# The rotary embedding's row exchange in a hybrid decoder layer: by small SBUF transfers instead of a product on TensorE

## The chip, the cores and the metric

The kernel runs on one core of one Trainium2 chip. The metric is the device time in microseconds (us) of one execution; the time shown for a kernel is the median of several executions.

## The reference

One decoder layer on a sequence of 512 tokens with 1024 features, all in float32: a SwiGLU half step, a mixer, a second SwiGLU half step, a final RMSNorm. The mixer projects the normalised input once, runs a gated delta rule (GDN, 4 heads of 128) beside a sparse attention (8 query heads in 2 key groups, head size 64), and joins them in an output projection. Queries and the keys of two of the three attention branches get a partial rotary embedding on their first 16 features:

```python
def partial_rope(x, pos):
    half = ROPE_DIM // 2          # 8
    ...
    x1, x2 = xr[..., :half], xr[..., half:]
    rot = jnp.concatenate([x1 * cos - x2 * sin, x2 * cos + x1 * sin], axis=-1).astype(x.dtype)
    return jnp.concatenate([rot, x[..., ROPE_DIM:]], axis=-1)
```

## The kernel before

Features lie on the 128 partitions and tokens on the free axis. Five engine programs (TensorE as PE, VectorE as DVE, ScalarE as ACT, GpSimd as POOL, SyncE as SP for the loads) run side by side and meet at semaphores. Each engine executes its own list strictly in order. Large products are made of three TensorE passes on split operands (`three_pass`, L592 to L594).

The mixer has three parts. First come seven full projection steps (`pe_projection`). Then comes a mixed stretch whose order is written out in `SCHEDULE`: 14 half projection tiles (`pe_half(n, g)`, each cut into three groups g) alternate with the rounds of the GDN's chunk algorithm (`pe_gdn`, jobs with names such as `g_arg`, `rb`, `kk`, `c1`, `y1`, `t1`, `u1`, `k_tok`, `v_tok`, `vn0`, `s0`, `o`). The third part is the attention. In the mixed stretch the half tiles are there so that TensorE has work while another engine brings the result of a GDN job out of PSUM for the next one.

GDN jobs write to three PSUM banks in turn. A job waits until the job three before it has been evacuated (`gdn_bank_free`). So `v_tok` of the fourth token tile waits for the evacuation of `t4` (DVE, L2250), since the jobs in between are `u4` and `v_tok` of the third tile.

Six tiles are rotated: r = 0, 1 are the two keys (`z[:, 0]`, `z[:, 1]`), r = 2 to 5 the four query tiles (`nq`). A rotated tile holds two groups of 64 features, of which the first 16 are rotated. The source tile r is written by DVE at the end of half tile r + 4 (`dve_half_end`, L1505 or L1507, which signals `proj_evac`). The rotation stands in the schedule behind group 1 of half tile r + 5:

- TensorE multiplies the source with a constant 128 x 128 permutation `rope_swap` (`pe_rope`, L1520). It exchanges rows 0 to 7 with rows 8 to 15 of each group, with a minus sign on one of the two, and gives zero in all other rows. The result lies in bank r % 2.
- DVE makes source x cos (`dve_rope`, L1526), then bank x sin into `z[:, 2 + r % 2]` (L1530), then the sum of both (L1533).
- Half tiles 6 to 11 on TensorE wait (`rope_b`) until L1530 has read that bank.

The constant cos is 1 and sin is 0 outside of the rotated rows. The step on SP that matters here is `sp_mixer`: loads of weight tiles, of eight pieces of the compression weights (L1323), and of the output weights (L1356, L1360). ACT rounds a half tile's weights in `act_half_split` (L1388), and DVE makes the rest in `dve_half_split` (L1394). In front of `SCHEDULE`, ACT copies three constants to bfloat16 (L2428 to L2430).

Of the kernel before, what the change touches and what calls it, by code (L numbers as in the profile page):

```python
# [270 lines left out]
def build(nc, dram, out):  # L271
    with ExitStack() as ctx:
# [4 lines left out]
        def sem(name):  # L277
            return ctx.enter_context(nc.semaphore(name))
# [228 lines left out]
        kqv_ready = sem("kqv_ready")  # L507
        kqv_sq = sem("kqv_sq")
        l2_done = sem("l2_done")
        rope_mm = sem("rope_mm")  # L510
        rope_a = sem("rope_a")
        rope_b = sem("rope_b")
        rope_ready = sem("rope_ready")
# [811 lines left out]
        def sp_mixer(sp):  # L1325
            for m in range(FULL_STEPS):
                step = MIX0 + m
                sp.wait_ge(lo_ready, step - 1)
                if FULL_KIND[m] == "small":
                    sp.dma_start(raw[:, m % 2, 0:KT * P], dram["w_small"]).then_inc(raw_landed[m % 2], 16)  # L1330
                else:
                    sp.dma_start(raw[:, m % 2, :], dram["w_in"][FULL_TILE[m], :, :])\
                      .then_inc(raw_landed[m % 2], 16)
            for s in range(HALF_STEPS):
                par = HALF_LOAD[s][0]
                if s < 2:
                    sp.wait_ge(lo_ready, HALF0 + s - 1)
                elif s == 2:
                    sp.wait_ge(half_lo, 2)
                else:  # L1340
                    sp.wait_ge(half_lo, 2 * s)
                sp.dma_start(raw[:, par, :], dram["w_in"][HALF_TILE[s], :, :]).then_inc(raw_landed[par], 16)
                for piece in {2: (0, 1), 3: (2, 3, 4), 4: (5, 6, 7)}.get(s, ()):
                    if piece == 0:
                        sp.wait_ge(half_lo, 4)
                    elif piece >= 2:
                        sp.wait_ge(cmp_done, piece - 1)
                    sp_cmp(sp, piece)
            for o in range(OUT_STEPS):
                if o < RING:  # L1350
                    sp.wait_ge(cmp_done, 2 * CMP_STEPS) if o == 0 else sp.wait_ge(half_lo, HALVES_N)
                else:
                    sp.wait_ge(lo_ready, splits(OUT0 + o) - 1)
                here = raw[:, o % 2, :].rearrange("p (b k n) -> p b k n", b=2, k=KT)
                rows = dram["w_out"][o, :, :].rearrange("p (b k n) -> p b k n", b=2, k=KT)
                sp.dma_start(here[:, :, 0:4, :], rows[:, :, 0:4, :]).then_inc(raw_landed[o % 2], 16)  # L1356
                for g in range(2):
                    for r in range(2):
                        for b in range(2):
                            sp.dma_start(half_of(here, g)[:, b, 4 + r:8:2, :],  # L1360
                                         rows[r * NSA_DH:(r + 1) * NSA_DH, b, 4 + 2 * g:6 + 2 * g, :])\
                              .then_inc(wout_landed[o % 2], 16)
# [79 lines left out]
        def pe_half(pe, n, g):  # L1442

            if g == 0:
                pe.wait_ge(half_lo, n + 1)
                if n == 0:
                    pe.wait_ge(proj_evac, CONV_EVACS - 2)
                if n in (2, 3):
                    pe.wait_ge(v_evac, n - 1)
                elif n in (4, 5):  # L1450
                    pe.wait_ge(cmp_in_ready, 2 * (n - 3))
                elif n >= 6:
                    pe.wait_ge(proj_evac, CONV_EVACS + n - 5)
                if 6 <= n <= 11:
                    pe.wait_ge(rope_b, n - 5)
            a, b = KGROUPS[g]
            if n < 2:
                for t, k in V_ORDER[2 * a:2 * b]:
                    if n == 0 and (t, k) == (0, 0):
                        pe.wait_ge(proj_evac, CONV_EVACS)  # L1460
                    tok, w = slice(t * P, (t + 1) * P), slice((4 * n + k) * 2 * P, (4 * n + k + 1) * 2 * P)
                    mm = three_pass(pe, banks[t][:, 0:2 * P], h_hi[:, 4 * n + k, tok], h_lo[:, 4 * n + k, tok],
                                    w_hi[:, 1, w], w_lo[:, 1, w], n == 0 and k == 0, n == 1 and k == 3)
                if b == KT:
                    mm.then_inc(half_done, 1)
                return
            for k in range(a, b):
                mm = three_pass(pe, banks[n % 2][:, :], *slot_w(1, (n % 2) * KT + k), h_hi[:, k, :], h_lo[:, k, :],
                                k == 0, k == KT - 1)
            if b == KT:  # L1470
                mm.then_inc(half_done, 1)
# [40 lines left out]
            if n + 2 < HALVES_N:  # L1512
                dve_half_split(dve, n + 2)

        def rope_bank(r):
            return banks[r % 2]

        def pe_rope(pe, r):
            pe.wait_ge(proj_evac, CONV_EVACS + r + 1)
            pe.matmul(rope_bank(r)[:, :], const("rope_swap"), rope_source(r)[0],  # L1520
                      start=True, stop=True).then_inc(rope_mm, 1)

        def dve_rope(dve, r):
            src, dst = rope_source(r)
            dve.wait_ge(proj_evac, CONV_EVACS + r + 1)
            dve.tensor_tensor(dst, src, const("cos"), ALU.mult).then_inc(rope_a, 1)  # L1526
            dve.wait_ge(rope_mm, r + 1)
            if r >= 2:
                dve.wait_ge(rope_ready, r - 1)
            dve.tensor_tensor(z[:, 2 + r % 2, :], rope_bank(r)[:, :], const("sin"), ALU.mult).then_inc(rope_b, 1)  # L1530
            dve.wait_ge(rope_a, r + 1)
            dve.wait_ge(rope_b, r + 1)
            dve.tensor_tensor(dst, dst, z[:, 2 + r % 2, :], ALU.add).then_inc(rope_ready, 1)  # L1533

        def act_projection(act):
            for m in range(FULL_STEPS):
# [857 lines left out]
        def pe_mixer(pe):  # L2394
            pe_projection(pe)
            for what, *n in SCHEDULE:
                if what == "half":
                    pe_half(pe, *n)
                elif what == "scalars":
                    pe_scalars(pe)  # L2400
                elif what == "rope":
                    pe_rope(pe, *n)
                elif what == "cmp":
                    pe_cmp(pe, *n)
                elif what == "hid_sum":
                    pe_hid(pe)
                elif what == "kcvc":
                    pe_kcvc(pe)
                elif what == "scores":
                    pe_scores(pe, *n)  # L2410
                elif what == "cmp_pt":
                    pe_cmp_pt(pe, *n)
                elif what == "att":
                    pe_attention(pe, *n)
                elif what == "gdn":
                    for tt, name in ROUNDS[n[0]]:
                        pe_gdn(pe, tt, name)
            pe_out(pe)

        def act_mixer(act):  # L2420
            act_split(act, MIX0 + 1)
            act.wait_ge(rest_landed, 48)
            act_rms(act, 1)
            act_r(act, 1)
            act_projection(act)
            act_scalars_end(act)
            act_gdn(act, 0, "g_arg")
            act.activation(ident_bf[:, :], ident, ACT.Copy).then_inc(consts_bf, 1)  # L2428
            act.activation(neg_causal_bf[:, :], const("neg_causal"), ACT.Copy).then_inc(consts_bf, 1)
            act.activation(zero_bf[:, :], ident, ACT.Copy, scale=0.0).then_inc(consts_bf, 1)  # L2430
            for what, *n in SCHEDULE:
                if what == "half_end":
                    act_half_end(act, *n)
                elif what == "hid_sum":
                    act_hid_parts(act)
                    act_hid(act)
                elif what == "softmax" and n[0] == 2:
                    act_cmp_exp(act)
                elif what == "cmp_pt":
                    act_cmp_pt(act, *n)  # L2440
                elif what == "gdn_rms":
                    act_gdn_rms(act)
                elif what == "att":
                    act_attention(act, *n)
                elif what == "gdn":
                    for tt, name in ROUNDS[n[0]]:
                        if (tt, name) != (0, "g_arg"):
                            act_gdn(act, tt, name)
            act_out(act)
            act_ffn_start(act, 1)  # L2450
# [30 lines left out]
        def pool_mixer(pool):  # L2481
# [3 lines left out]
            pool.memset(hid_v, 0.0).then_inc(pads_set, 1)  # L2485
            pool.memset(bdv, 0.0).then_inc(pads_set, 1)
            pool.memset(state, 0.0).then_inc(state_ready, 1)
            for what, *n in SCHEDULE:
                if what == "att":
                    pool_scale(pool, *n)  # L2490
# [199 lines left out]
```

## Time and profile before

| | |
|---|---|
| median of 3 executions | 1116.54 us (1116.14 to 1116.83) |
| the profiled execution's own time | 1116.19 us |
| its span in the trace | 1114.4 us |
| PE busy | 1082.6 us, 97% |
| DVE, ACT, POOL busy | 778.0, 446.5, 443.5 us |
| mean granted TensorE clock | 0.989 |

The span is what the profiler records between the first and the last instruction; 1.8 us of the execution's time lie around it. All positions below are us from the start of the span. Busy shares are averages over stages with different limits. A wait is put down to the engine whose signal came last.

### The profile page before, as it was taken

What the parts mean: (1) busy time and instruction counts of PE and PEld (TensorE: products, weight loads), DVE (VectorE), ACT (ScalarE), POOL (GpSimd) and SP (SyncE); (2) the same over time, 40 slices, a digit from 0 to 9 for tenths busy, and PEclk for the clock granted to TensorE, in tenths of its full rate; (3) what the DMA queues carried; (4) which work ended last, traced back from release to release, by engine and by line L of the source; (5) the groups of instructions that cost most, each with busy time, mean ns of one, the idle gap of its engine ahead of it and who ended that gap; (6) DMA issues with size and microseconds to landing.
All of it is one profiled execution on the core that took longest, in us unless ns stands there. A gap on an engine that the chain in (4) does not pass through costs nothing.

```text
span 1114.4 us, 20141 instructions
## 1 busy us (share of the span) xinstructions
PE 1082.6 (97%) x8484; PEld 938.2 (84%) x8484; DVE 778.0 (70%) x941; ACT 446.5 (40%) x639; POOL 443.5 (40%) x281
## 2 busy tenths in 40 slices
PE   6899999999999999999999999999999999999996
PEld 5799899988998888887787667888898899989986
DVE  5998379946987566653566487566997389837964
ACT  6534244423435334311214566343453145413432
POOL 0663169505833000312300389433480279306912
PEclk9999999999999999999999899999999999999999
DMA  6244233333232222113103001123133323422222
GB/s 228 77 124 151 76 94 99 116 108 103 89 112 95 87 103 76 40 58 134 39 28 86 4 1 39 36 79 103 59 104 115 111 77 114 135 92 80 101 85 76
DMA packets 34590, 98.45 MB, mean 88 GB/s; under 512 B 3664, under 2 KB 10320, under 8 KB 32848
## 3 DMA queue, kind: packets, MB, share of 16 engines
q1 hardware_dynamic: 34224, 97.26, 26.7%
q8 instruction: 57, 0.93, 0.3%
q14 instruction: 21, 0.17, 0.0%
q10 hardware_dynamic: 288, 0.08, 0.0%
HBM read 95.24 MB, written 2.10 MB: 87 GB/s over the span
## 4 chain that ended last, share of the span: by engine, by line
PE 87%; DVE 8%; ACT 3%; issue 2%; DMA 0%; POOL 0%; DVEq 0%; ACTq 0%
PE bank L592 25%; PE bank L594 24%; PE bank L593 24%; PE bank L2131 3%; PE bank L1917 1%; PE bank L1884 1%; PE bank L1905 1%; DVE hb_lo L716 1%; DVE w_lo L1020 1%; PE bank L2183 1%; DVE cv L1611 1%; DVE w_lo L1097 1%; PE bank L2180 1%; PE bank L1716 1%; PE bank L1520 1%
## 5 line engine op out<-in xcount | busy, mean ns | idle before, releaser
L592 PE MATMUL bank<-hb_hi,w_hi 128*128 128x256 f32 x1064 | 295.5, 278 | 6.9 <-DVE w_lo L1097 3.6
L594 PE MATMUL bank<-hb_hi,w_lo 128*128 128x256 f32 x1064 | 294.7, 277 | 0.0
L593 PE MATMUL bank<-hb_lo,w_hi 128*128 128x256 f32 x1064 | 294.7, 277 | 0.0
L592 PEld LDWEIGHTS bank<-hb_hi,w_hi 128*128 128x128 f32 x1064 | 200.5, 188 | 8.7 <-DVE w_lo L1097 4.5
L593 PEld LDWEIGHTS bank<-hb_lo,w_hi 128*128 128x128 f32 x1064 | 200.5, 188 | 0.3
L594 PEld LDWEIGHTS bank<-hb_hi,w_lo 128*128 128x128 f32 x1064 | 200.6, 189 | 0.0
L592 PE MATMUL bank<-act_hi,w_hi 128*128 128x512 f32 (+1 forms) x460 | 180.4, 392 | 10.0 <-DVE w_lo L1033 9.8
L593 PE MATMUL bank<-act_lo,w_hi 128*128 128x512 f32 (+1 forms) x460 | 179.8, 391 | 0.0
L594 PE MATMUL bank<-act_hi,w_lo 128*128 128x512 f32 (+1 forms) x460 | 179.6, 391 | 0.0
L1014 ACT ACTIVATE w_hi<-raw 128x1536 fp32r<-128x1536 f32 (+1 forms) x67 | 108.7, 1622 | 161.1 <-PE bank L594 161.1
L1020 DVE TENSOR_TENSOR w_lo<-raw,w_hi 128x1536 fp32r<-128x1536 f32 (+1 forms) x67 | 159.2, 2376 | 15.8 <-ACT w_hi L1014 15.3
L1047 POOL TENSOR_TENSOR w_sum<-raw 128x512 f32<-128x512 f32 x34 | 58.5, 1720 | 250.0 <-PE bank L594 220.1
L1097 DVE TENSOR_TENSOR w_lo<-w_sum,w_hi 128x1024 fp32r<-128x1024 f32 x76 | 114.1, 1503 | 9.4 <-POOL w_sum L1051 9.2
L1083 ACT ACTIVATE w_hi<-w_sum 128x1024 fp32r<-128x1024 f32 x76 | 80.2, 1058 | 88.4 <-POOL w_sum L1052 74.4
L592 PEld LDWEIGHTS bank<-act_hi,w_hi 128*128 128x128 f32 x460 | 87.0, 189 | 29.9 <-DVE w_lo L1033 9.8
L592 PE MATMUL bank<-h_hi,w_hi 128*128 128x512 f32 x264 | 109.9, 416 | 0.0
L594 PE MATMUL bank<-h_hi,w_lo 128*128 128x512 f32 x264 | 105.0, 398 | 0.0
L593 PE MATMUL bank<-h_lo,w_hi 128*128 128x512 f32 x264 | 105.0, 398 | 0.0
L594 PEld LDWEIGHTS bank<-act_hi,w_lo 128*128 128x128 f32 x460 | 86.9, 189 | 19.9
L593 PEld LDWEIGHTS bank<-act_lo,w_hi 128*128 128x128 f32 x460 | 86.9, 189 | 19.3
L1220 DVE SCALAR_TENSOR_TENSOR x<-bank,x 128x512 f32<-128x512 f32 x46 | 29.6, 686 | 102.2 <-PE bank L594 102.2
L1051 POOL TENSOR_TENSOR w_sum<-raw,w_sum 128x512 f32<-128x512 f32 x34 | 78.5, 2308 | 2.7
(307 smaller groups left out, 1702.6 us busy)
## 6 DMA issues: line engine op xcount, KB each, us to landing
raw<-in_gate_up SPq DMA_DIRECT2D x43, 1024.0 KB, 5.4
raw<-in_w_in SPq DMA_DIRECT2D x13, 1024.0 KB, 4.9
raw<-in_down SPq DMA_DIRECT2D x8, 1024.0 KB, 5.1
raw<-in_down SPq DMA_DIRECT2D x16, 512.0 KB, 4.1
raw<-in_down SPq DMA_DIRECT2D x8, 768.0 KB, 4.3
raw<-in_w SPq DMA_DIRECT2D x8, 512.0 KB, 3.8
x<-in_x SPq DMA_DIRECT2D x4, 512.0 KB, 7.5
raw<-in_w_out SPq DMA_DIRECT2D x4, 512.0 KB, 4.6
```

Of the source, the lines that this page charges most:

```text
L592: pe.matmul(out_ap, wh, xh, start=first, stop=False)
L593: pe.matmul(out_ap, wh, xl, start=False, stop=False)
L594: return pe.matmul(out_ap, wl, xh, start=False, stop=last)
L716: dve.tensor_tensor(hb_lo[:, b], HB_RAW[b], hb_hi[:, b].bitcast(F32), ALU.subtract).then_inc(hb_lo_dve, 1)
L1014: act.activation(w_hi[:, par, 0:cols], raw[:, par, 0:cols], ACT.Copy).then_inc(hi_ready, 1)
L1020: dve.tensor_tensor(w_lo[:, par, 0:cols], raw[:, par, 0:cols], w_hi[:, par, 0:cols].bitcast(F32), ALU.subtract).then_inc(lo_ready, 1)
L1047: pool.tensor_tensor(S[0], A[3], A[2], ALU.add).then_inc(s_sum, 1)
L1051: pool.tensor_tensor(S[3], A[0], S[1], ALU.subtract).then_inc(s_sum, 1)
L1083: act.activation(w_hi[:, st.step % 2, c], w_sum[:, st.step % 2, c], ACT.Copy).then_inc(s_hi, 1)
L1097: dve.tensor_tensor(w_lo[:, par, c], w_sum[:, par, c], w_hi[:, par, c].bitcast(F32), ALU.subtract).then_inc(s_lo, 1)
L1220: dve.scalar_tensor_tensor(x[:, k, :], banks[4 * (st.step % 2) + ab][:, :], 0.5, x[:, k, :], ALU.mult, ALU.add).then_inc(x_added, 1)
L2131: mm = pe.matmul(o[ch, q, :], a, b, start=True, stop=True)
```

## The change

The permutation product goes. SP copies the rows of the source tile within SBUF instead: four transfers for each r, each of 8 partitions with 2 KB (512 float32). They are issued in `sp_mixer` between the weight loads: r = 0 behind compression piece 2, r = 1 behind piece 4, r = 2 and 3 behind piece 7, r = 4 and 5 behind the load of the next tile. Each waits for the source (`proj_evac`), the first two for a cleared target, the later ones for the rotation two before.

The target is `z[:, 2 + r % 2]`, which POOL clears once with two memsets of 128 x 512 at the start of the mixer, the second of them behind the small transposes (`small_t`). DVE then multiplies this tile with sin in place. The minus sign, which was in the permutation, is put into the constant sin: ACT multiplies two blocks of 8 partitions x 512 by -1, directly behind its three bfloat16 copies. The wait of half tiles 6 to 11 for `rope_b` goes.

```diff
@@ sp_mixer
                     sp_cmp(sp, piece)
+                    if piece == 2:
+                        sp_rope(sp, 0)
+                for r in {3: (1,), 4: (2, 3), 5: (4, 5)}.get(s, ()):
+                    sp_rope(sp, r)
@@ pe_half
-                if 6 <= n <= 11:
-                    pe.wait_ge(rope_b, n - 5)
@@
-        def pe_rope(pe, r):
-            pe.wait_ge(proj_evac, CONV_EVACS + r + 1)
-            pe.matmul(rope_bank(r)[:, :], const("rope_swap"), rope_source(r)[0],
-                      start=True, stop=True).then_inc(rope_mm, 1)
+        def sp_rope(sp, r):
+            src, swapped = rope_source(r)[0], z[:, 2 + r % 2, :]
+            sp.wait_ge(proj_evac, CONV_EVACS + r + 1)
+            if r < 2:
+                sp.wait_ge(rope_cleared, r + 1)
+            else:
+                sp.wait_ge(rope_ready, r - 1)
+            for g in range(2):
+                a, b, c = [g * NSA_DH + i * ROPE_DIM // 2 for i in range(3)]
+                sp.dma_start(swapped[a:b], src[b:c]).then_inc(rope_swapped[r % 2], 16)
+                sp.dma_start(swapped[b:c], src[a:b]).then_inc(rope_swapped[r % 2], 16)
 
         def dve_rope(dve, r):
             src, dst = rope_source(r)
             dve.wait_ge(proj_evac, CONV_EVACS + r + 1)
             dve.tensor_tensor(dst, src, const("cos"), ALU.mult).then_inc(rope_a, 1)
-            dve.wait_ge(rope_mm, r + 1)
-            if r >= 2:
-                dve.wait_ge(rope_ready, r - 1)
-            dve.tensor_tensor(z[:, 2 + r % 2, :], rope_bank(r)[:, :], const("sin"), ALU.mult).then_inc(rope_b, 1)
+            swapped = z[:, 2 + r % 2, :]
+            dve.wait_ge(rope_swapped[r % 2], 64 * (r // 2 + 1))
+            if r == 0:
+                dve.wait_ge(sin_signed, 2)
+            dve.tensor_tensor(swapped, swapped, const("sin"), ALU.mult).then_inc(rope_b, 1)
             dve.wait_ge(rope_a, r + 1)
             dve.wait_ge(rope_b, r + 1)
-            dve.tensor_tensor(dst, dst, z[:, 2 + r % 2, :], ALU.add).then_inc(rope_ready, 1)
+            dve.tensor_tensor(dst, dst, swapped, ALU.add).then_inc(rope_ready, 1)
@@ act_mixer, behind the copy into zero_bf
+            for g in range(2):
+                first = slice(g * NSA_DH, g * NSA_DH + ROPE_DIM // 2)
+                act.activation(const("sin")[first], const("sin")[first], ACT.Copy, scale=-1.0).then_inc(sin_signed, 1)
@@ pool_mixer
+            pool.memset(z[:, 2, :], 0.0).then_inc(rope_cleared, 1)
+            pool.wait_ge(small_t, 1)
+            pool.memset(z[:, 3, :], 0.0).then_inc(rope_cleared, 1)
```

## Rows read from the trace of the kernel before

**Rows 1.** The page: busy time of each engine, and the chain by engine.

```profile
PE 1082.6 (97%) x8484; PEld 938.2 (84%) x8484; DVE 778.0 (70%) x941; ACT 446.5 (40%) x639; POOL 443.5 (40%) x281
...
PE 87%; DVE 8%; ACT 3%; issue 2%; DMA 0%; POOL 0%; DVEq 0%; ACTq 0%
```

**Rows 2.** Windows: stretch, its length, busy PE, PEld, DVE, ACT, POOL, clock, DMA.

```profile
505.50:523.00 17.50, 17.50 (x302) 13.80 (x298) 5.37 (x8) 3.86 (x6) 1.04 (x1) 1.00 0.43 153
```

**Rows 3.** The chain in order of time, 503 to 590: start, us, what.

```profile
505.61 1.06 PE bank L1520 x2
...
573.46 0.86 PE bank L1520 x2
```

**Rows 4.** Timeline of DVE, 497 to 589: start, us, what.

```profile
497.53 0.68 DVE L1505 TENSOR_TENSOR z<-bank,r_sb 128x512 f32<-128x512 f32 x1
...
506.86 0.68 DVE L1530 TENSOR_TENSOR z<-bank,consts 128x512 f32<-128x512 f32 x1
...
579.86 0.68 DVE L1507 SCALAR_TENSOR_TENSOR nq<-bank,r_sb 128x512 f32<-128x512 f32 x1
...
587.68 0.69 DVE L1530 TENSOR_TENSOR z<-bank,consts 128x512 f32<-128x512 f32 x1
```

**Rows 5.** Timelines of POOL, DVE and PE around rotation 1, 524 to 538.

```profile
524.39 1.68 POOL L2286 TENSOR_TENSOR sq_sum<-lt,level_c 128x512 f32<-128x512 f32 x1 [1.67 <-DVE lt L2242]
...
529.43 1.03 POOL L2320 TENSOR_TENSOR state_dec<-state,e_sums 128x512 f32<-128x512 f32 x1
...
537.15 1.27 POOL L2286 TENSOR_TENSOR cm<-lt,level_c 128x512 f32<-128x512 f32 x1 [2.03 <-PE bank L2131]
...
524.83 1.80 DVE L1526 TENSOR_TENSOR nk_rot<-z,consts 128x512 f32<-128x512 f32 x1
...
530.56 0.69 DVE L2274 TENSOR_TENSOR state<-state_dec,bank 128x512 f32<-128x512 f32 x1 [2.25 <-POOL state_dec L2320]
...
531.77 0.32 PE L2180 MATMUL bank<-state,kqv 128*64 128x128 f32 x1
```

**Rows 6.** Timelines of DVE and PE around rotation 4, 573 to 579.

```profile
573.07 0.69 DVE L2260 TENSOR_TENSOR kbg<-bank,t_s_kbg 128x512 f32<-128x512 f32 x1 [4.27 <-PE bank L2170]
...
577.46 0.68 DVE L2250 TENSOR_TENSOR tinv<-tinv,bank 128x512 f32<-128x512 f32 x1
...
577.67 1.18 PE L2172 MATMUL bank<-consts,kqv 128*128 128x128 f32 x8
```

**Rows 7.** Timelines of ACT, DVE and PE, 456 to 461.

```profile
456.08 0.62 ACT L2195 ACTIVATE h_raw<-h_raw 128x512 f32<-128x512 f32 x1
456.60 0.30 ACT L2428 ACTIVATE ident_bf<-consts 128x128 bf16<-128x128 f32 x1
...
457.20 1.04 ACT L1388 ACTIVATE w_hi<-raw 128x1024 fp32r<-128x1024 f32 x1
...
458.27 1.23 DVE L1394 TENSOR_TENSOR w_lo<-raw,w_hi 128x1024 fp32r<-128x1024 f32 x1 [1.64 <-ACT w_hi L1388]
...
460.15 0.65 PE L2170 MATMUL bank<-consts,kqv 128*128 128x128 f32 x4 [2.65 <-DVE lt L2239]
```

**Rows 8.** Windows around TensorE's pause at 457.5 (columns as in rows 2).

```profile
457.50:460.20 2.70, 0.05 (x2) 0.05 (x1) 1.82 (x2) 0.74 (x1) 0.32 (x1) 1.00 0.00 0
...
461.00:462.00 1.00, 1.00 (x6) 1.00 (x6) 1.00 (x2) 0.00 (x0) 1.00 (x1) 0.50 0.00 0
```

**Rows 9.** Timeline of SP's queue, landing times of line L1360, and ACT's next split.

```profile
581.70 0.33 SPq L1342 DMA_DIRECT2D raw<-in_w_in  x1
...
582.71 0.61 SPq L1360 DMA_DIRECT2D raw<-in_w_out  x1
...
DMA to landing us min/median/max: 2.3/3.4/5.8
...
592.51 1.05 ACT L1388 ACTIVATE w_hi<-raw 128x1024 fp32r<-128x1024 f32 x1
```

**Rows 10.** Timeline of POOL, 355 to 625: its first work behind its memsets.

```profile
450.09 1.04 POOL L2296 TENSOR_TENSOR h_raw<-neg_c,gcl 128x512 f32<-128x512 f32 x1 [87.48 <-DVE gcl L1661]
```

More of the change, by code:

```diff
@@ L509, in build @@
         l2_done = sem("l2_done")
-        rope_mm = sem("rope_mm")
+        rope_swapped = [sem("rope_swapped_%d" % i) for i in range(2)]
+        rope_cleared = sem("rope_cleared")
+        sin_signed = sem("sin_signed")
         rope_a = sem("rope_a")
@@ L1513, in dve_half_end @@
                 dve_half_split(dve, n + 2)
-        def rope_bank(r):
-            return banks[r % 2]
-        def pe_rope(pe, r):
-            pe.wait_ge(proj_evac, CONV_EVACS + r + 1)
-            pe.matmul(rope_bank(r)[:, :], const("rope_swap"), rope_source(r)[0],
-                      start=True, stop=True).then_inc(rope_mm, 1)
+        def sp_rope(sp, r):
[9 more added lines that the diff above has]
+                sp.dma_start(swapped[b:c], src[a:b]).then_inc(rope_swapped[r % 2], 16)
         def dve_rope(dve, r):
@@ L2400, in pe_mixer @@
                     pe_scalars(pe)
-                elif what == "rope":
-                    pe_rope(pe, *n)
                 elif what == "cmp":
```

## The prediction

> **What bounds the kernel now.** I read the page first: PE is busy 97% of the span, and the chain that ended last runs over PE for 87% of it [rows 1]. That is an average, so I looked at the stretch in which the six rotations lie, 497 to 589 us. The windows show it full: in the 17.5 us from 505.5, PE is busy for 17.50 us at full clock, DVE for 5.37 us [rows 2]. The chain in order of time names PE without a gap there, and the six permutation products stand in it, each as two instructions [rows 3]. The waits of PE by themselves name nothing in this stretch, the wait for `rope_b` neither, so dropping that wait gives nothing by itself. Going backwards, the one real pause of PE in the mixed stretch is at 457.5: 2.65 us, ended by DVE's L2239 [rows 7]. The added ACT work lands exactly in front of it.
>
> **What is removed: six products.** In the chain rotation 0 takes 1.06 us [rows 3]. The six pieces are 1.06, 1.06, 1.05, 1.06, 0.86 and 1.06 (first and fifth are shown), 6.15 us in all. That is the ceiling. What survives of it depends on the next thing that PE needs from another engine behind each of them. I went through the PE jobs behind each product, with the evacuation that frees their bank:
>
> - Rotations 0, 2, 3 and 5: the next DVE, ACT or POOL result is ready more than 0.5 us before PE would come for it with the product gone. Their pieces survive: 1.06 + 1.05 + 1.06 + 1.06 = 4.23 us.
> - Rotation 1: PE's job `vn1` (L2180) starts at 531.77 and needs the state, which DVE finishes at 530.56 + 0.69 = 531.25. DVE waited for POOL's `state_dec`, done at 530.46. POOL worked without a pause from 524.39 [rows 5]. This chain began at PE's `g_arg` job, ahead of the product, so it doesn't move up with it. PE would come at 530.71 and find the state at 531.25: only 0.52 us of the 1.06 are slack. And the sine product now reads two SBUF tiles in the middle of this POOL chain. The nearest row is the cosine product, which reads two SBUF tiles: 1.80 us here beside POOL, while POOL's L2286 takes 1.68 us; alone, the same POOL operation takes 1.27 us [rows 5]. So one such DVE product costs POOL about 0.4 us. I take 0.52 - 0.4 = 0.1 us of gain. Bounds: 0.52 if the sine product disturbs nothing as now, and -0.5 if it costs POOL about 1 us.
> - Rotation 4: DVE works through from 573.07 (four evacuations of `k_tok`, the three rotation products, then L2250, done at 577.46 + 0.68 = 578.14). The eight L2172 of PE are two jobs of four, 1.18 us from 577.67, so the second starts near 578.25; it needs the bank that L2250 frees [rows 6]. The slack is 0.1 us. DVE's string starts at `k_tok`, ahead of the product, and is no shorter than before. So 0.1 us of the 0.86 survives. What is late next is DVE, not PE. Bounds: 0.1 and 0.86.
>
> The rule that fits rotation 1 is in the Trainium skill, page "SBUF — State Buffer", section "Who interferes with whom": a DVE instruction with two SBUF inputs contends with a GpSimd instruction that reads SBUF, one with a single SBUF input doesn't. The trace agrees for the cosine product (1.80 us beside POOL). By that rule rotation 1 gives about 0.1 us; if moving the input from PSUM to SBUF made no difference, it would give 0.52 us.
>
> Sum of the gains: 4.23 + 0.1 + 0.1 = 4.4 us, between 3.8 and 5.6.
>
> **What is added on ACT: 1.04 us on the path.** ACT's 128 x 512 operation at 456.08 is followed by the next at 456.60, 0.52 us later. An 8 x 512 operation isn't in the trace. From below it costs what a short one costs, 0.2 us from start to start (three 128 x 128 copies fill 456.60 to 457.20 [rows 7]); from above 0.52. Each partition has the same 512 elements to pass, so I take 0.52, twice: 1.04 us. They stand behind the copy to `zero_bf`. Queued behind them on ACT is L1388 (the rounding of half tile 2, at 457.20), on which DVE's L1394 waits (1.64 us), behind it in DVE's list L2239, and for that one PE waits 2.65 us before L2170 [rows 7]. ACT is busy without a gap before. So PE's pause grows by the whole 1.04 us, bounds 0.4 and 1.04. Nothing hides it.
>
> **The clock behind that pause.** From 460.9 the granted clock is 0.50, the lower of its two levels (1.2 GHz): 0.50 at 461 to 462, after the pause of 457.5 to 460.2 [rows 8]. I count no change: the longer pause is 3.7 us, PE comes back at 461.2, and the slow spell that follows is taken as it is. If it gets longer, see the rivals.
>
> **What is added on SP and in the DMA queue: hidden.** The trace has no transfer from SBUF to SBUF, and none of 16 KB. Issue costs 0.33 us (L1342) to 0.61 us (L1360); landing of the 64 KB transfers is 2.3 us at best, 3.4 in the median, 5.8 at worst [rows 9]. Four issues and one landing make, from the source's end: 4 x 0.33 + 2.3 = 3.6 us, or 4 x 0.61 + 5.8 = 8.2 us at worst; with 0.61 and 3.4 it is 5.8 us. I take about 4 us, since a fourth of the bytes should not land later. What is available is the time from the end of the source to the start of L1530: 506.86 - 498.21 = 8.65 us for r = 0, 587.68 - 580.54 = 7.1 us for r = 5 [rows 4]; the other four have 8.6 to 16.8 us. So DVE doesn't wait. If r = 5 took the worst value, DVE would wait 1.1 us, behind it are the score masks, and PE has more than 8 us of other work. For the loads: SP's waits for the sources end before the ones that the next weight loads have anyway, save for r = 5. Its four issues end at 580.54 + 1.3 to 2.4 = 581.9 to 583.0, and the load of 581.70 goes out up to 1.3 us later, and the output weights behind it (L1356, L1360). ACT takes that tile at 592.51 [rows 9], 11 us after; the output weights are needed only after the attention. Cost: nothing.
>
> **What is added on POOL, and on DVE.** Two memsets at about 362 and 391 us; POOL has nothing to do until 450.09 and has idled 87.48 us by then [rows 10]. They cost nothing. DVE's three products for each rotation stay, with 0.68 us for the sine product from PSUM [rows 4].
>
> **The sum.** -4.4 + 1.04 = -3.4 us. The profiled execution took 1116.19 us (span 1114.4 and 1.8 around it), so it would come to 1112.8 us. The median is 0.35 us above the profiled execution; carried over, 1116.54 - 3.4 = 1113.2 us. A difference of 0.2%, 2.2 us, is about what a measurement of this kernel can tell from no change; below 1114.3 is faster.
>
> **The rivals.**
>
> 1. *All six products come off the time*, and ACT's operations are short: -6.15 + 0.4 = -5.7 us, 1110.8 us. For it speaks the gapless chain of PE. Against it speak the two places with 0.52 and 0.1 us of slack.
> 2. *The pause makes the slow spell longer.* The rows show the clock at 0.50 right after a pause of 2.65 us, and it is back at 1.00 by 466; a slow spell of about 3.4 us with PE full costs half of it, 1.7 us. If the longer pause draws one more of these, the net is -3.4 + 1.7 = -1.7 us, 1114.9 us, within 0.2%. Against it: PE is dense right behind the pause, and had recovered from one of 2.65 us. The Trainium skill, page "TensorE: Matmul & The Clock Gate", calls the throttled state the default that activity releases, and warns of idle gaps; that speaks for this rival.
> 3. *The savings are given back.* The stretch is paced by DVE and its bank releases in more places than I found, so that only half of 4.23 us is left and rotation 1 turns to -0.5: -2.1 - 0.1 + 0.5 + 1.04 = -0.7 us, 1115.9 us.
> 4. *The other side: slower, by late transfers.* If the last of four transfers lands L us after the source, DVE stalls at the sine product. Rotation 4 decides: it has 13.1 us, and DVE's string behind it goes straight into PE's job, so every us beyond is lost. Rotations 2, 3 and 5 have 8.6, 10.9 and 7.1 us and some 3 to 4 us of cover behind. At L = 13 almost nothing is lost, from about 13.5 us on the 3.4 us of gain are gone, and at L = 15 the loss is 9 us, which gives 1122 us. Against it: the worst landing shown makes 8.2 us.
>
> **How the numbers follow.** My forecast 0.62, with its own range 1112.3 to 1114.4 (rotation 4's 0.76 and rotation 1's 0.4 below, ACT's 0.6 below; rotation 1's -0.5 and some 0.6 for a place overlooked above). Rival 1: 0.09. Rival 2: 0.13. Rival 3: 0.12. Rival 4: 0.04. The range 1111.7 to 1115.6 leaves out rival 1, rival 4 and about half of rival 3: 0.19. Faster by over 0.2%: nearly all of the forecast, and rival 1: 0.69. Within: the forecast's rest, rivals 2 and 3: 0.26. Slower: rival 4 and a tail of rival 3: 0.05.
>
> **What would show it.** The row L1520 is gone. PE's pause at L2170 reads about 3.7 us, not 2.65. PE has a new wait of 0.5 us or more at L2180 behind rotation 1, ended by DVE's L2274, which waits for POOL; and one of 0.7 us at L2172 behind rotation 4, ended by L2250. DVE has no wait for DMA at the sine product. The new transfers show 0.3 to 0.6 us each to issue and 2 to 3.5 us to land. I am wrong if DVE waits at the sine product, if the slow spell behind 460 lasts well over 3.4 us, or if PE's waits behind rotations 0, 2, 3 and 5 are above 0.2 us.

## The result, and the profile after

The changed kernel took 1110.4 us in the median, the kernel before 1116.4 us beside it: ratio 0.995, 95% interval 0.9931 to 0.9968. It is faster, but by more than forecast: 1113.2 us was said, and 1110.4 lies below the range of 1111.7 to 1115.6. (One execution of six, 1508.86 us at a mean granted clock of 0.655, is left out.) The profiled execution took 1109.73 us.

The page of the kernel after; [rows 1] has the same lines of before:

```profile
span 1107.9 us, 20148 instructions
...
PE 1074.0 (97%) x8472; PEld 935.5 (84%) x8472; DVE 779.8 (70%) x941; ACT 448.1 (40%) x641; POOL 445.0 (40%) x283
...
PE 87%; DVE 8%; ACT 3%; issue 2%; POOL 1%; DMA 0%; DVEq 0%; ACTq 0%; POOLq 0%
```

The spans differ by 6.5 us. L1520 is gone; most lines stand 9 further down (L2170 is now L2179). The waits of PE from 440 to 640, before:

```profile
PE bank L2170 <- DVE lt L2239: 2.6, 1, 2.6
PE bank L1884 <- ACT p_att L1971: 1.7, 1, 1.7
```

and after (us in total, times, longest):

```profile
PE bank L2179 <- DVE lt L2248: 3.9, 1, 3.9
PE bank L1893 <- ACT p_att L1980: 1.7, 1, 1.7
PE bank L2189 <- DVE state L2283: 1.1, 1, 1.1
PE bank L2181 <- DVE tinv L2259: 0.7, 1, 0.7
```

The three waits that were forecast are there (3.9, 1.1 and 0.7 us), and no other new one above 0.2 us. The 1.7-us wait stands at the start of the attention, before and after. The cause of the first, in ACT's timeline, as in [rows 7]:

```profile
455.04 0.62 ACT L2204 ACTIVATE h_raw<-h_raw 128x512 f32<-128x512 f32 x1
...
456.16 1.26 ACT L2440 ACTIVATE consts<-consts 8x512 f32<-8x512 f32 x2
457.45 1.06 ACT L1394 ACTIVATE w_hi<-raw 128x1024 fp32r<-128x1024 f32 x1
```

From `h_raw` to the rounding of the half tile it is 457.45 - 455.04 = 2.41 us; it was 457.20 - 456.08 = 1.12 us. The two operations cost 1.29 us.

Around rotation 1, POOL and then DVE, as in [rows 5]:

```profile
526.36 1.62 POOL L2316 TENSOR_TENSOR uinv<-ident_c,sq_sum 128x512 f32<-128x512 f32 x1
...
529.64 1.48 POOL L2329 TENSOR_TENSOR state_dec<-state,e_sums 128x512 f32<-128x512 f32 x1
...
525.04 1.79 DVE L1534 TENSOR_TENSOR nk_rot<-z,consts 128x512 f32<-128x512 f32 x1
526.75 1.76 DVE L1539 TENSOR_TENSOR z<-z,consts 128x512 f32<-128x512 f32 x1
528.62 1.60 DVE L1542 TENSOR_TENSOR nk_rot<-nk_rot,z 128x512 f32<-128x512 f32 x1
531.23 0.69 DVE L2283 TENSOR_TENSOR state<-state_dec,bank 128x512 f32<-128x512 f32 x1 [1.00 <-POOL state_dec L2329]
```

The same stretch of the kernel before, where the sine product still read PSUM (POOL, then DVE):

```profile
526.15 1.61 POOL L2307 TENSOR_TENSOR uinv<-ident_c,sq_sum 128x512 f32<-128x512 f32 x1
...
526.55 0.67 DVE L1530 TENSOR_TENSOR z<-bank,consts 128x512 f32<-128x512 f32 x1
```

The sine product, 0.68 us in the other places, takes 1.76 us in the changed kernel. POOL's operation beside it is no slower than before (1.62 against 1.61 us), but the sum now starts later and lies beside `state_dec`: 1.48 us, where it was 1.03. The state starts 531.23 - 524.61 = 6.62 us after the first POOL operation of the chain (L2295, 524.61), before 530.56 - 524.39 = 6.17 us: 0.45 us later.

SP's queue at rotation 5 (z<-nq are the new transfers), which stands beside [rows 9], and DVE's products that use them:

```profile
579.14 0.62 SPq L1528 DMA_DIRECT2D z<-nq  x1
...
581.14 0.62 SPq L1529 DMA_DIRECT2D z<-nq  x1
581.81 0.44 SPq L1344 DMA_DIRECT2D raw<-in_w_in  x1
...
585.65 0.68 DVE L1534 TENSOR_TENSOR nq_rot<-nq,consts 128x512 f32<-128x512 f32 x1
586.25 0.68 DVE L1539 TENSOR_TENSOR z<-z,consts 128x512 f32<-128x512 f32 x1
```

Each issue takes 0.62 us or a little more. DVE goes from L1534 to L1539 without a pause here and in the five other rotations.

**Where the 6.5 us lie.** I use three landmarks: A, ACT's first `h_raw` of the GDN (456.08 before, 455.04 after); B, DVE's last `state` of the GDN; C, the start of ACT's first `h_hi` in the attention. Before:

```profile
622.72 0.69 DVE L2274 TENSOR_TENSOR state<-state_dec,bank 128x512 f32<-128x512 f32 x1 [0.39 <-PE bank L2183]
...
647.64 0.59 ACT L1979 ACTIVATE h_hi<-bank 128x512 fp32r<-128x512 f32 x1
```

After:

```profile
620.25 0.69 DVE L2283 TENSOR_TENSOR state<-state_dec,bank 128x512 f32<-128x512 f32 x1 [0.39 <-PE bank L2192]
...
641.19 0.59 ACT L1988 ACTIVATE h_hi<-bank 128x512 fp32r<-128x512 f32 x1
```

Up to A the changed kernel gains 1.04 us, from A to B 1.43 us (166.64 to 165.21), from B to C 3.98 us (24.92 to 20.94). Together that is 6.45 us, and behind C nothing. All six products lie between A and B, so most of the gain is in a stretch that the edit doesn't touch. The windows (columns as in [rows 2]) say what happens there, before:

```profile
631.00:642.00 11.00, 10.84 (x62) 6.17 (x61) 5.22 (x27) 5.40 (x30) 7.19 (x13) 0.53 0.01 3
```

and after:

```profile
631.00:642.00 11.00, 10.83 (x94) 6.13 (x92) 9.14 (x38) 9.01 (x37) 10.19 (x16) 1.00 0.02 4
```

Before, the granted clock (third column from the end) is at its lower level for 10.2 us there, and the count of PE's matmuls in the window is 62 instead of 94. After, no slow spell follows the 1.7-us pause at L1893. Likewise the kernel before has a spell of 3.4 us at 392 that the changed one hasn't, worth 1.55 us by the operations on both sides of it. Before, and after:

```profile
392.00:396.00 4.00, 4.00 (x13) 3.12 (x12) 3.93 (x5) 0.00 (x0) 0.00 (x0) 0.57 0.28 53
...
392.00:396.00 4.00, 4.00 (x18) 3.23 (x18) 3.72 (x5) 0.17 (x1) 0.00 (x0) 1.00 0.28 66
```

The changed kernel has 6.8 us instead of 3.4 at 460. Its spell at 54 is longer too, and it is 0.51 us behind by 70 us; but the second execution of the kernel before, which has no spell at 54, is 0.26 us behind there as well, so this isn't shown to be the clock's. The spell at 460 in the changed kernel:

```profile
459.00:466.00 7.00, 5.58 (x25) 5.51 (x26) 4.86 (x8) 1.87 (x5) 3.79 (x3) 0.51 0.00 0
```

Did the edit move the spells, or do they fall differently in each execution? That was the question for the experiments.

### The profile page after: what moved, and what is told of

The parts are those of the page before. It is cut to its first block, busy times and chain, and to the rows that moved or that the text cites. A ratio compares the mean times of both kernels' runs of the same rounds, so it can differ in the third digit from the quotient of the medians.

```text
span 1107.9 us, 20148 instructions
## 1 busy us (share of the span) xinstructions
PE 1074.0 (97%) x8472; PEld 935.5 (84%) x8472; DVE 779.8 (70%) x941; ACT 448.1 (40%) x641; POOL 445.0 (40%) x283
## 4 chain that ended last, share of the span: by engine, by line
PE 87%; DVE 8%; ACT 3%; issue 2%; POOL 1%; DMA 0%; DVEq 0%; ACTq 0%; POOLq 0%
PE bank L594 25%; PE bank L595 24%; PE bank L596 24%; PE bank L2140 3%; PE bank L1926 1%; PE bank L1893 1%; PE bank L1914 1%; DVE hb_lo L718 1%; DVE w_lo L1022 1%; DVE cv L1620 1%; PE bank L2192 1%; DVE w_lo L1099 1%; PE bank L2189 1%; DVE x L961 1%; DVE c_sb L1155 0%
```

## The experiments

**1 and 2. Both kernels again.** No edit.

> The changed kernel once more. The two traces show 6.5 us between the spans, but only 2.5 us of it arise between 455 and 621 us; 1.55 us are a slow-clock spell at 392 us that is there before and not after, and 4.0 us a slow-clock spell of 10.2 us at 631 us (start of the attention) that is there before and not after. Theory A (the clock spell is a matter of where the program happens to stand against the clock's own rhythm): runs scatter over 1108 to 1114 us, the mean granted clock goes with the time (0.994 fast, 0.989 slow), and some executions have the spell at the attention's start. Theory B (the change itself removes it): all executions within 0.3%, and no spell there in any.

> The kernel before once more, for a second trace. Theory A: another trace has its slow-clock spells in other places or of other lengths, and a time near 1112 us is possible when the spell at 631 us is missing. Theory B: the spell of about 10 us at 631 us is there again, time 1116 to 1117 us.

Measured later: the changed kernel 1112.5 us (12 executions, 1109.6 to 1121.1), ratio 0.9994 (0.9972 to 1.0016); the kernel before, timed against itself, 1116.6 us, ratio 1.0028 (1.0009 to 1.0047). The 35 executions of the kernel before that both are compared with have a median of 1115.05 us. So the changed kernel's second median is 2.1 us above its first and inside the forecast's range. So a 0.28% difference of a kernel from itself came out with an interval that excludes none: the interval is narrower than what the comparison can tell. The second profiled execution of the kernel before has a span of 1111.2 us, 3.2 less than the first, with the same waits: no spell at 54 or 392, and 6.8 instead of 10.2 us of it in the attention. From B to C the difference is 1.74 us. The spells differ between executions of one kernel. The changed kernel's second profile has none in the attention either, but three of its twelve executions have a mean granted clock of 0.984 to 0.986 and take 1115.8 to 1119.8 us, where its two profiled ones, at 0.991 and 0.993, take 1109.7 and 1109.6. So the changed kernel does have more slow clock in some executions. Over all executions it has a mean of 1112.7 us (17) and the kernel before 1116.1 us (85): 3.4 us less, 95% interval 1.4 to 5.3.

**3. ACT's two operations alone, on the kernel before.** They copy the blocks onto themselves, so the constant keeps its values.

```diff
+            for g in range(2):
+                first = slice(g * NSA_DH, g * NSA_DH + ROPE_DIM // 2)
+                act.activation(const("sin")[first], const("sin")[first], ACT.Copy).then_inc(sin_signed, 1)
```

> The kernel before with only the two added ACT operations of 8 x 512 (here with scale 1, so that the constant keeps its value). Forecast's theory: the pause of TensorE in front of L2170 grows from 2.65 us by 1.04 us; the changed kernel's trace says by 1.25 us (3.9 us). Rival: with it the slow-clock spell behind the pause is longer by another 1 us, so 2.3 us in all by 475 us, unless it is made up at the attention's start. Time 1117.5 to 1118.8 us if the spell at 631 us stays, about 1114.5 us if it goes.

Measured: 1117.4 us, ratio 1.0029 (1.0013 to 1.0044), which by itself is no more than that of the kernel before against itself. The wait decides:

```profile
PE bank L2173 <- DVE lt L2242: 3.9, 1, 3.9
```

The pause grows from 2.6 to 3.9 us with nothing else changed. A to B takes 167.71 us, 1.07 and 1.24 us more than in the two executions of the kernel before, with a 3.4-us spell in all three. The attention has 6.8 us of slow clock here.

**4. The sign operations put off** until ACT is through with its work for the first half tile.

```diff
-            for g in range(2):
-                first = slice(g * NSA_DH, g * NSA_DH + ROPE_DIM // 2)
-                act.activation(const("sin")[first], const("sin")[first], ACT.Copy, scale=-1.0).then_inc(sin_signed, 1)
@@ half_end
+                    if n[0] == 0:
+                        for g in range(2):
+                            first = slice(g * NSA_DH, g * NSA_DH + ROPE_DIM // 2)
+                            act.activation(const("sin")[first], const("sin")[first], ACT.Copy, scale=-1.0).then_inc(sin_signed, 1)
```

> The changed kernel with the two sign operations moved behind ACT's first half-tile split, where ACT idles for 5 us. Theory: the pause of TensorE is back at 2.6 us, and the kernel is 1.2 us faster than the changed one, 2.3 us if the slow spell gets shorter too: 1108 to 1109 us at an equal clock at the attention's start. Rival (the longer pause is what removes the spell at the attention's start): the spell of 10 us is back and the time is 1111 to 1113 us.

Measured: 1111.7 us, ratio 0.9971 (0.9952 to 0.9989). The pause is back at 2.6 us:

```profile
PE bank L2179 <- DVE lt L2248: 2.6, 1, 2.6
```

The time is above the 1108 to 1109 us that were expected, since in this execution no spell followed the pause but one of 10.2 us lay in the attention. That is also what the rival of this experiment said (the longer pause keeps the attention's spell away). Experiments 3 and 5 speak against it: both have the longer pause and a spell in the attention, of 6.8 and 10.2 us.

**5. Without the transfers.** It leaves the row exchange out: `sp_rope` is gone and DVE multiplies what stands in the tile.

```diff
-                    if piece == 2:
-                        sp_rope(sp, 0)
-                for r in {3: (1,), 4: (2, 3), 5: (4, 5)}.get(s, ()):
-                    sp_rope(sp, r)
@@ dve_rope
-            dve.wait_ge(rope_swapped[r % 2], 64 * (r // 2 + 1))
+            if r < 2:
+                dve.wait_ge(rope_cleared, r + 1)
+            else:
+                dve.wait_ge(rope_ready, r - 1)
```

> The changed kernel without the 24 transfers within SBUF (it leaves the row exchange out; the sine product takes the cleared tile). Theory: the transfers are hidden. From ACT's exponential in front of its bfloat16 copies (near 455 us) to the fourth z tile (near 619 us) the distance is the same as in the changed kernel, 164.1 us, to 0.2 us, at equal clock spells. Rival: issuing and landing cost something on DVE or delay loads, and the distance is shorter by 0.5 us or more.

Measured: 1113.7 us, one execution. `w_lo` of half tile 6, ahead of the rotations, to B takes 120.88 us, in the changed kernel 120.86, and A to B 165.03 and 165.21. So the transfers cost 0.2 us at most, and nothing from half tile 6 on. The memsets are still in it. And with the same order on PE and the same 6.8 us of slow clock at 460 as in the changed kernel, this execution has a spell in the attention:

```profile
629.00:640.00 11.00, 11.00 (x64) 5.98 (x62) 5.29 (x27) 5.58 (x29) 6.84 (x13) 0.53 0.01 4
```

So a program timed like the changed one up to there can get this spell, and its absence in the changed kernel's two profiles isn't the edit's fixed effect.

**6. Rotations 1 and 4 moved on DVE** (with 4's edit), out of POOL's chain and out of the string in front of L2259.

```diff
-                    dve_rope(dve, *n)
+                    if n[0] not in (1, 4):
+                        dve_rope(dve, *n)
@@
+                if (what, *n) == ("gdn", 18):
+                    dve_rope(dve, 1)
+                elif (what, *n) == ("half_end", 9):
+                    dve_rope(dve, 4)
```

> sign_later with the DVE part of rotation 1 moved behind round 18 and that of rotation 4 behind half tile 9's end, where DVE idles. Theory (products 1 and 4 were given back because DVE's string stood in front of the state update and the bank release): TensorE's waits of 1.1 us (state) and 0.7 us (L2259) go, and the stretch from 498 to 597 us gets 1.1 + 0.7 = 1.8 us shorter than in sign_later. Rival (POOL's chain and DVE's evacuations alone set these places): the waits stay at 0.5 us or more. Time: 1.8 us less than sign_later at an equal clock, about 1110 us in the median.

Measured: 1112.5 us, ratio 0.9956 (0.9937 to 0.9976). Both waits are gone, and half tile 6 to B is 118.78 us, 2.10 less than in experiment 4 (120.88); 1.8 was expected from the two waits. With DVE's three products out of the way POOL runs through the chain at the short durations, shorter than in the kernel before too, where the cosine product stood beside it:

```profile
524.59 1.28 POOL L2316 TENSOR_TENSOR uinv<-ident_c,sq_sum 128x512 f32<-128x512 f32 x1
...
527.07 1.03 POOL L2329 TENSOR_TENSOR state_dec<-state,e_sums 128x512 f32<-128x512 f32 x1
```

The median of 1112.5 us misses the 1110 that were expected. The profiled execution, 1112.4 us, had 13.7 us of slow clock in the attention:

```profile
624.00:638.00 14.00, 14.00 (x78) 7.82 (x77) 6.65 (x34) 7.12 (x36) 9.34 (x16) 0.51 0.01 3
```

**7 and 8. The pauses filled.** Products that nobody reads go into PE's two pauses, on experiment 4's kernel, and on experiment 6's.

```diff
+                if i == 2:
+                    for _ in range(7):
+                        pe.matmul(t_bank(0)[:, :], zero_bf[:, :], per_head(ident_bf[:, :]), start=True, stop=True)
@@ pe_gdn
+            if (tt, name) == (0, "k_tok"):
+                pe.wait_ge(e_ready, 1)
+                for _ in range(20):
+                    pe.matmul(banks[7][:, 2 * P:4 * P], h_hi[:, 0, 0:P], h_hi[:, 0, 0:2 * P], start=True, stop=True)
```

> sign_later with TensorE work that nobody reads in its two pauses: 20 products of 256 columns in front of the job that waited 2.6 us near 460 us, 7 bfloat16 products of 512 columns at the attention's third slot, where it waited 1.7 us. Theory: the pauses bring the slow-clock spells at 460 and 610 to 640 us, and these make most of the scatter; with the pauses filled no spell stands there in the trace, the mean granted clock is 0.993 or more in most executions, and the median is 2 to 3.5 us below sign_later, 1108 to 1110 us, with less scatter. Rival: the spells come from the sparse work behind the pauses, not from the pauses; they stay, and the time stays at 1111 to 1112 us.

> rope_moved and filled together: if both theories hold, 1.8 us and 2 to 3.5 us below sign_later, 1106 to 1108 us in the median. If the clock theory fails, the same as rope_moved, about 1110 us.

Measured: 1106.6 us, ratio 0.9916 (0.9891 to 0.9942), and 1105.2 us, ratio 0.9914 (0.9884 to 0.9944). In both profiles no spell follows either pause. Experiment 7's six executions lie within 1106.1 to 1107.9 us; their mean is 4.6 us below that of experiment 4 (95% interval 3.4 to 5.9), more than the 2 to 3.5 expected. The clock over the attention's start in experiment 7:

```profile
624.00:640.00 16.00, 15.55 (x128) 8.73 (x126) 11.90 (x54) 13.37 (x60) 13.48 (x21) 1.00 0.01 2
```

Experiment 8 has the lowest median of the study, 1.3 us below experiment 7, but its six executions reach from 1103.8 to 1111.0 us, so the two aren't told apart by their times. A to B they differ by 2.07 us (table below).

**9 and 10. The change priced with both pauses filled**: the kernel before with 20 fillers and 7, the changed one (sign operations where they were) with 30, for its longer pause, and 7.

> The kernel before, with 20 products of 256 columns that nobody reads put into PE's pause of 2.6 us at L2170 and 7 of 512 columns into its 1.7-us pause at the second slot of the attention. With both pauses filled no stretch of slow clock should follow 460 or the attention's start in the profiled execution, and the scatter between executions should shrink. Theory (the change itself is worth 2.5 us: 3.73 of products taken off, 1.25 of the longer pause given back): 1106.6 (the filled kernel with the sign operations put off) + 3.73 = 1110.3 us. Rival (the change itself keeps the spells away): the fillers do less here, the spells stay, and the time stays above 1113.

> The changed kernel, its sign operations where they were, with 30 such products in its pause of 3.9 us and the same 7 at the attention's second slot. The pair with the kernel before and its fillers prices the change with the spells taken from both. Theory: 498 to the last state update 3.73 us shorter than in that kernel, the stretch ahead of it 1.25 us longer, the whole 2.5 us shorter (about 1107.8 us). Rival, the forecast's own sum: 3.4 us shorter. Rival, the change takes the spells away by itself: the difference stays near 6 us.

Measured: 1111.8 us (10 executions), ratio 0.9956 (0.9940 to 0.9973), and 1108.8 us (6), ratio 0.9933 (0.9909 to 0.9956). Expected were 1110.3 and 1107.8 us. The means differ by 2.8 us (95% interval 1.0 to 4.7), which speaks against 6 but doesn't tell 2.4 from the forecast's 3.4. The landmarks do. A and B of the kernel before with fillers (ACT, then DVE):

```profile
457.28 0.62 ACT L2202 ACTIVATE h_raw<-h_raw 128x512 f32<-128x512 f32 x1
...
622.39 0.69 DVE L2281 TENSOR_TENSOR state<-state_dec,bank 128x512 f32<-128x512 f32 x1 [0.39 <-PE bank L2190]
```

and of the changed kernel with them:

```profile
454.81 0.62 ACT L2211 ACTIVATE h_raw<-h_raw 128x512 f32<-128x512 f32 x1
...
617.49 0.69 DVE L2290 TENSOR_TENSOR state<-state_dec,bank 128x512 f32<-128x512 f32 x1 [0.39 <-PE bank L2199]
```

The windows around the filled pause at 460, of the first and of the second:

```profile
455.00:469.00 14.00, 13.93 (x158) 12.52 (x155) 9.82 (x17) 6.91 (x15) 6.17 (x5) 1.00 0.05 8
...
455.00:469.00 14.00, 13.82 (x144) 12.01 (x142) 9.05 (x15) 5.75 (x12) 6.18 (x5) 1.00 0.12 32
```

With the clock at 1.00 from A to C in both, A to B takes 165.11 us before and 162.68 us after; in experiment 7, with the sign operations put off, 161.37. So the products are worth 3.74 us, ACT's operations cost 1.31 us, and the change gives 2.43 us. B to C is 20.93 and 20.92 us. The rest of the 4.8 us between these spans, 2.47 us, lies ahead of A. There the first has spells at 54 and 392, which the fillers don't reach, and the second has none; but the kernel before with the same two spells reaches A 1.20 us earlier (456.08), at an equal clock, so about half of the 2.47 us isn't the clock's. It arises ahead of 115 us, and I haven't traced it.

The stretches of all twelve profiles, in us; "slow" is how long the clock was at its lower level in the stretch:

| kernel | A to B | slow | B to C | slow |
|---|---|---|---|---|
| before | 166.64 | 3.4 | 24.92 | 10.2 |
| before again | 166.47 | 3.4 | 23.18 | 6.8 |
| ACT's operations alone | 167.71 | 3.4 | 23.17 | 6.8 |
| changed | 165.21 | 6.8 | 20.94 | 0 |
| changed again | 164.24 | 3.4 | 20.91 | 0 |
| without transfers | 165.03 | 6.8 | 25.05 | 10.2 |
| sign operations put off | 161.38 | 0 | 24.95 | 10.2 |
| rotations 1 and 4 moved | 160.82 | 3.4 | 25.95 | 13.7 |
| sign operations put off, filled | 161.37 | 0 | 20.92 | 0 |
| rotations moved, filled | 159.30 | 0 | 20.92 | 0 |
| before, filled | 165.11 | 0 | 20.93 | 0 |
| changed, filled | 162.68 | 0 | 20.92 | 0 |

## Why the prediction was wrong

**The step that failed is the term for the clock, put at nothing: "I count no change", with the sum taken off one profiled execution ("The profiled execution took 1116.19 us").** The prediction looked only at the spell at 460, whose pause the edit touches. That execution also held 10.2 us of slow clock in the attention and 3.4 us at 392, which it didn't name. The changed kernel's had neither. The two account for 3.98 us, from B to C, and 1.55 us. In the sum of the two traces: 3.36 us forecast, 0.93 less from the edit itself, 1.00 less between A and B from the longer spell at 460, 0.51 less ahead of A, and 5.53 more from the two spells that are gone, make the 6.45 us. Experiments 1, 2 and 5 show that spells differ between executions of one kernel and can follow programs timed alike. The first timing of the kernel before, all within 1115.7 to 1117.0 us, had hidden that; 85 executions reach from 1111.8 to 1126.5. Part of the miss is luck: the changed kernel's first median, 1110.4 us of five executions, wasn't met again (1112.5 us of twelve). The range held terms for ACT and for the rotations, and none for a clock that gives time back; rival 2 let it only lose.

**The edit itself gives 2.4 us, less than the 3.4 forecast.** So the time fell by more than forecast and the edit is worth less than forecast; only the executions without spells show the second.

- *Rotations 0, 2, 3 and 5:* forecast 4.23 us. Followed from landmark to landmark the four gave 1.05, 0.87, 0.85 and 1.04 us, 3.81 in all. PE has no wait above 0.2 us behind them, as said. What took 0.4 us at rotations 2 and 3 I haven't traced.
- *Rotation 1:* forecast 0.1 us gained. It is 0.08 us lost. The mechanism is the one forecast, contention of DVE's products with POOL, by another way: the sine product doesn't slow the POOL operation beside it further, it becomes slow itself, and the sum behind it then meets `state_dec`. That cost 0.45 us, 0.4 was taken, and PE waits 1.1 us. The Trainium skill, page "SBUF — State Buffer", section "Who interferes with whom", has GpSimd share its ports with DVE's second pair; the 1.76 us of the sine product beside POOL against 0.68 us elsewhere agrees.
- *Rotation 4:* forecast 0.1 us, measured 0.00; what is late is L2259 (L2250 before), with the 0.7 us of wait said. Together the products gave 3.74 us where 4.4 were forecast.
- *ACT:* forecast 1.04 us, measured 1.25 to 1.31 by the pause, the timeline and the filled pair, 1.07 and 1.24 from A to B in experiment 3. The mechanism was right and the size was short: an operation of 8 x 512 runs 0.62 us, as long as one of 128 x 512 (0.62 us), and the pair got none of the overlap that I had read from 456.08 to 456.60. Experiments 3 and 4 turn this wait on and off.
- *Transfers and memsets:* hidden, as forecast (experiment 5 for the transfers; for the memsets, the second profile of the kernel before and experiment 10's of the changed one, both without a spell up to there, reach A at 454.77 and 454.81 us). An issue costs 0.62 us in most cases, just above the 0.3 to 0.6 that was said, and 0.79 at most. The trace gives no landing time for them, so the 2 to 3.5 us stay untested.

**The rivals.** Rival 1 (all products off) is refuted by the waits of 1.1 and 0.7 us; that its 1110.8 us came nearest to the measured 1110.4 is luck. Rival 2's longer spell at 460 did come in one profile of the changed kernel (6.8 us) and not in the second (3.4 us). Over the eight profiles with unfilled pauses, the four with the 3.9-us pause have 6.8, 3.4, 3.4 and 6.8 us there, the four with the 2.6-us pause 3.4, 3.4, 3.4 and 0. That points the rival's way, but eight profiles are too few to settle it. Rival 3 is partly right, with 0.4 us given back in places I had overlooked. Rival 4 didn't occur.

**What stays open:** whether the edit changes the odds of a spell. Its two profiles have none in the attention; the profiles of the four variants without fillers (ACT's operations alone, sign operations put off, no transfers, rotations moved) have one each, of 6.8 to 13.7 us. By the mean granted clock of each execution, 0.9901 in the changed kernel's 17 and 0.9893 in the 79 of the kernel before that have one, the changed kernel spends 2.0 us less at the lower level (each execution's time there is 2 x (1 - clock) x span); the interval, 1.3 us more to 5.2 us less, takes in no difference. A line fitted through these 96 executions, with slow time and the kernel as its terms, puts the edit at equal clock at 2.8 us (1.6 to 4.0), in agreement with the 2.4 of the landmarks.

## What to carry to other kernels

Before a change of a few us is summed against a profiled execution, look for slow stretches of the clock in it and take a second profile: a spell that lies there by chance is worth as much as the change. To price such a change, compare the distance between two landmarks around it in executions whose clock is full throughout, and fill PE's pauses in both kernels with products that nobody reads if the spells don't go away otherwise. ACT's operation on 8 partitions took as long as one on 128 (0.62 us each), so work of a few partitions isn't small: ask first what is queued behind it.

## What the runs showed of the hardware

- A pause of PE of only 1.7 us, with thin work around it, was followed by 0, 6.8, 10.2 or 13.7 us at the lower level of the clock (1.2 GHz), and differently in two executions of one kernel. With seven unread products in that pause, none of the four profiles had such a spell. With those and the twenty in the pause at 460, the ratio to the kernel before fell from 0.9971 (experiment 4) to 0.9916 (experiment 7). The Trainium skill, page "TensorE: Matmul & The Clock Gate", section "What's actually happening", calls the throttled state the default that activity releases; that agrees with what the fillers did.
- A transfer of 16 KB from SBUF to SBUF on 8 partitions costs SP 0.62 us to issue, more than the 0.33 us of the 1 MB load in [rows 9] (0.44 us in the changed kernel's row).
- Beside POOL's chain, DVE's three operations that read two SBUF tiles take 1.79, 1.76 and 1.60 us, where the same ones take 0.68 to 0.72 elsewhere; POOL's take 1.62, 1.74 and 1.48 us, where they take 1.28, 1.28 and 1.03 without them (experiment 6). The sine product that reads PSUM took 0.67 us beside POOL in the kernel before.
